# Where the mean, the second pair's products and four centred tiles of a two-block network are kept

## The chip, the cores and the metric

The kernel runs on one core of one Trainium2 chip. The metric is the device time of one execution in microseconds (us), the median of the runs shown. TensorE (PE), VectorE (DVE), ScalarE (ACT), GpSimd (POOL) and SyncE (SP, which issues the transfers) each work off their own list of instructions in order, and meet through semaphores.

## What is computed

512 rows of width 1024 go through a network of two blocks in float32. Cut to what the change touches, the first block's layer, run twice, is:

```
h   = x @ w_in                      # then three mixers: attention, latent attention, RWKV
mix = concatenate([o_sb, o_mla, o_rwkv]) @ w_o
x   = layer_norm(ALPHA * x + mix, ln1_g, ln1_b)
u_act, u_gate = split(x @ ffn_w_up)
x   = layer_norm(ALPHA * x + (gelu(conv(u_act)) * u_gate) @ ffn_w_down, ln2_g, ln2_b)
```

The second block has a recurrent mixer, a pooling mixer and two feed-forward nets behind RMS norms.

## The kernel before

**Layout.** Features lie on the 128 partitions and the 512 rows of x along the free axis, so x is 8 tiles of 128x512. Weights stream from HBM as chunks of 128x1024 (eight 128x128 blocks), in a fixed order, into two slots of `raw`. Each product is made of three passes: a chunk is split by ACT into a high part `wh` (L1560) and by DVE into a low part `wl` (L2392), x likewise into `xh` and `xl`, and `split_product` issues xh·wh, xl·wh, xh·wl (L673 to L675). One chunk is 24 matmuls of 128x512 and one PSUM bank of output. Chunks alternate between the dense banks `dbank[0]` and `dbank[1]`; six more banks are `aux[0]` to `aux[5]`. `bank_free[j]` counts the reads that have freed dense bank j, `lo_done` the chunks whose low part is there, `pe_chunk` the chunks multiplied.

**Norms.** k = 0 to 8 number the norms: 0 and 1 are the layer norms of the first layer, 2 and 3 of the second, 4 to 8 the RMS norms. Norms 0, 1, 2 and 5 are "deferred" (`deferred`): the next product does not wait for the norm.
- `ahead_pair`: the first pair of chunks behind the norm is multiplied with the unnormalised x times the gain, as two parts `hidh`/`hidl` or `xh`/`xl` made by `ahead_hi` on ACT and `ahead_lo` on DVE (L2476), into `aux[0]` and `aux[1]`. After its first four tiles TensorE spreads the sum of x over all partitions (`spread`, L777: the mean, into `MEAN`), and later the sum of squares (into `aux[4]`). `ahead_out` corrects the products by mean and deviation afterwards.
- `turned_pair`: the second pair goes tile by tile over the normalised x, into `TURNED`, which is `(aux[3], dbank[1])`. Tile t waits until its low part is there: tiles 1, 3 and 5 get theirs from GpSimd (`low_parts`, L3354), the rest from DVE (L2527).
- The third pair follows in `turned_pair` too, in dbank[0] and dbank[1]. Its second product waits for all reads of bank 1.
- The fourth pair and the rest are plain `dense` calls.

**The norm's own work.** ACT copies the mean (L1613) to `mean_t` and squares it; DVE takes the mean off each of the 8 tiles (`centre`, L2453, reading the bank `MEAN`), makes the variance (L2443, L2444); ACT makes the root (L1620, L1622, into `aux[4]`, called RSTD). `turned_tiles` on DVE then scales tile by tile (L2517) while ACT makes `xh` (L1659) and the shifted x (L1662).

**The sums.** For norms 0 and 2 DVE adds up x (`tile_sum`, L2995) and its squares (`square_sum`, L3003) between the additions of the mixer's output (L3013), with one `ahead_lo` per tile among them; GpSimd splits four chunks of weights there (`low_weights`, L3361). For norms 1 and 3 GpSimd adds both up (`sum_tiles`, L3371 and L3377), and the squares of norm 5.

## Time and profile before

| | before |
|---|---|
| device time, median of 3 runs | 2390.69 us (2389.5 to 2391.33) |
| the profiled execution: its own time | 2391.46 us |
| the profiled execution: its span, first to last instruction | 2389.5 us |
| mean granted TensorE clock | 0.986 |
| PE busy | 2310.2 us (97%) |
| DVE busy | 1435.3 us (60%) |
| ACT busy | 1030.2 us (43%) |
| POOL busy | 253.8 us (11%) |
| DMA | 248.34 MB, mean 104 GB/s |

Matmuls are pipelined and their ends are modelled, so a busy PE is not PE at its peak. The idle time before an instruction is printed in brackets behind it, with what ended it. Norm 0 lies at 320 to 390 us of the span, norm 1 at 690 to 766, norm 2 at 1036 to 1105, norm 3 at 1430 to 1466, norm 5 at 1620 to 1672.

### The profile page before, as it was taken

What the parts mean: (1) busy time and instruction counts of PE and PEld (TensorE: products, weight loads), DVE (VectorE), ACT (ScalarE), POOL (GpSimd) and SP (SyncE); (2) the same over time, 40 slices, a digit from 0 to 9 for tenths busy, and PEclk for the clock granted to TensorE, in tenths of its full rate; (3) what the DMA queues carried; (4) which work ended last, traced back from release to release, by engine and by line L of the source; (5) the groups of instructions that cost most, each with busy time, mean ns of one, the idle gap of its engine ahead of it and who ended that gap; (6) DMA issues with size and microseconds to landing.
All of it is one profiled execution on the core that took longest, in us unless ns stands there. A gap on an engine that the chain in (4) does not pass through costs nothing.

```text
span 2389.5 us, 35656 instructions
## 1 busy us (share of the span) xinstructions
PE 2310.2 (97%) x13312; PEld 1852.6 (78%) x13312; DVE 1435.3 (60%) x1966; ACT 1030.2 (43%) x1608; POOL 253.8 (11%) x189
## 2 busy tenths in 40 slices
PE   8999999999998999999999998999999999999998
PEld 6777767888886777767888876777888888888887
DVE  4678687666576568686666556587444356533443
ACT  5667255333345657254333334665233243322332
POOL 0041110000042042110000040201000010000001
PEclk9999999999999999999999997999999999999999
DMA  4210014555432210014555431222322221222222
GB/s 161 80 62 28 29 45 158 194 193 193 160 111 72 82 63 28 29 45 159 192 194 193 160 111 39 79 90 97 98 96 96 97 97 62 89 97 97 97 97 88
DMA packets 68797, 248.34 MB, mean 104 GB/s; under 512 B 7632, under 2 KB 8144, under 8 KB 68688
## 3 DMA queue, kind: packets, MB, share of 16 engines
q1 hardware_dynamic: 68688, 246.85, 31.1%
q8 instruction: 72, 1.18, 0.2%
q14 instruction: 37, 0.30, 0.0%
HBM read 244.73 MB, written 2.10 MB: 103 GB/s over the span
## 4 chain that ended last, share of the span: by engine, by line
PE 84%; DVE 8%; ACT 4%; issue 3%; POOL 0%; DMA 0%; DVEq 0%; ACTq 0%; SPq 0%; POOLq 0%
PE dense L673 23%; PE dense L675 23%; PE dense L674 23%; PE aux L673 1%; ACT wh L1560 1%; PE aux L674 1%; PE aux L875 1%; PE aux L675 1%; DVE wl L2392 1%; PE aux L1033 1%; DVE hidl L2476 1%; PE aux L1051 1%; PE aux L1154 1%; PE aux L1165 1%; PE aux L1021 1%
## 5 line engine op out<-in xcount | busy, mean ns | idle before, releaser
L1560 ACT ACTIVATE wh<-raw 128x1024 fp32r<-128x1024 f32 x338 | 358.0, 1059 | 889.0 <-PE dense L675 880.5
L673 PE MATMUL dense<-xh,wh 128*128 128x512 f32 x1744 | 700.4, 402 | 29.4 <-DVE wl L2392 10.5
L675 PE MATMUL dense<-xh,wl 128*128 128x512 f32 x1744 | 682.6, 391 | 0.0
L674 PE MATMUL dense<-xl,wh 128*128 128x512 f32 x1744 | 682.4, 391 | 0.0
L2392 DVE TENSOR_TENSOR wl<-raw,wh 128x1024 fp32r<-128x1024 f32 x330 | 414.9, 1257 | 429.7 <-ACT wh L1560 428.8
L673 PEld LDWEIGHTS dense<-xh,wh 128*128 128x128 f32 x1744 | 329.8, 189 | 118.2 <-issue 42.8
L674 PEld LDWEIGHTS dense<-xl,wh 128*128 128x128 f32 x1744 | 330.0, 189 | 71.1 <-issue 5.8
L675 PEld LDWEIGHTS dense<-xh,wl 128*128 128x128 f32 x1744 | 329.4, 189 | 70.1
L673 PE MATMUL dense<-hidh,wh 128*128 128x512 f32 x928 | 362.9, 391 | 4.9 <-DVE hidl L2427 2.1
L674 PE MATMUL dense<-hidl,wh 128*128 128x512 f32 x928 | 361.2, 389 | 0.0
L675 PE MATMUL dense<-hidh,wl 128*128 128x512 f32 x928 | 361.1, 389 | 0.0
L673 PEld LDWEIGHTS dense<-hidh,wh 128*128 128x128 f32 x928 | 174.2, 188 | 46.6 <-DVE hidl L2427 7.4
L675 PEld LDWEIGHTS dense<-hidh,wl 128*128 128x128 f32 x928 | 174.2, 188 | 36.3
L674 PEld LDWEIGHTS dense<-hidl,wh 128*128 128x128 f32 x928 | 174.2, 188 | 35.7
L3258 DVE SCALAR_TENSOR_TENSOR x<-dense,mod,x 128x512 f32 (+1 forms) x64 | 48.1, 751 | 180.4 <-PE dense L675 180.4
L3377 POOL TENSOR_TENSOR norm_sq<-norm_sq,sq 128x512 f32<-128x512 f32 x38 | 69.1, 1817 | 722.1 <-ACT sq L1599 722.1
L3036 DVE CUSTOM_DVE_ANT_0 mraw<-mraw,cond 128x1024 f32<-128x1024 f32 x96 | 117.1, 1220 | 0.0
L2043 ACT ACTIVATE hidh<-hf 128x512 f32 (+1 forms) x108 | 68.1, 631 | 99.1 <-DVE hf L3234 92.7
L2427 DVE TENSOR_TENSOR hidl<-hf,hidh 128x512 f32 (+1 forms) x108 | 74.5, 690 | 59.8 <-ACT hidh L2043 59.8
L3371 POOL TENSOR_TENSOR norm_sum<-norm_sum,x 128x512 f32<-128x512 f32 x16 | 26.5, 1656 | 492.1 <-DVE x L2951 492.1
L1599 ACT ACTIVATE sq<-x 128x512 f32<-128x512 f32 x64 | 39.9, 624 | 44.5 <-DVE x L3013 16.2
L2693 DVE TENSOR_TENSOR_SCAN later<-keep 128x127 f32<-128x127 f32 (+3 forms) x32 | 34.0, 1062 | 17.1 <-ACT sig L1826 13.3
(450 smaller groups left out, 2669.2 us busy)
## 6 DMA issues: line engine op xcount, KB each, us to landing
raw<-stream SPq DMA_DIRECT2D x362, 512.0 KB, 3.4
mraw<-mod_stream SPq DMA_DIRECT2D x96, 512.0 KB, 4.2
x<-x_t SPq DMA_DIRECT2D x4, 512.0 KB, 6.7
y_t<-x SPq DMA_DIRECT2D x8, 256.0 KB, 2.0
cst<-consts SPq DMA_DIRECT2D x1, 994.0 KB, 9.3
band<-bands SPq DMA_DIRECT2D x1, 576.0 KB, 4.6
cond<-c_rows SPq DMA_DIRECT2D x1, 512.0 KB, 9.9
pv_next<-vecs SPq DMA_DIRECT2D x3, 82.5 KB, 4.6
```

The costliest lines, as they stand in the source:

```text
L673: pe.matmul(o, a, h, start=first, stop=False)
L674: pe.matmul(o, a, l, start=False, stop=False)
L675: return pe.matmul(o, b, h, start=False, stop=last)
L1560: act.activation(wh[:, slot].rearrange("p k m -> p (k m)"), raw[:, slot, :], ACT.Copy).then_inc(hi_done, 1)
L1599: act.activation(sq[:, m % 2, :], x[:, m, :], ACT.Square).then_inc(sq_ready, 1)
L2043: act.activation(hidh[:, slot_i, :], hf[:, j, :], ACT.Copy).then_inc(hidh_ready, 1)
L2392: tt(wl[:, slot].rearrange("p k m -> p (k m)"), raw[:, slot, :], wh[:, slot].rearrange("p k m -> p (k m)").bitcast(F32), SUB)\
L2427: tt(dst, src, hi.bitcast(F32), SUB).then_inc(ready, 1)
L2693: chain(dve.tensor_tensor_scan(later[:, b, 0:n - 1][:, ::-1], k, k, 1.0, MUL, ALU.min))
L3036: dve.tensor_tensor_reduce(mraw[:, j, :], mraw[:, j, :], cond[:], 1.0, 0.0, MUL, ADD, mod_col[:, m:m + 1])\
L3258: stt(x[:, m, :], dbank[j][:], mod[:, lay, bass.ds(40 + m, 1)], x[:, m, :], MUL, ADD).then_inc(bank_free[j], 1)
L3377: pool.tensor_tensor(norm_sq[:], norm_sq[:], sq[:, m % 2, :], ALU.add)\
```

## The change

It moves work between banks and engines; no product is added or left out.
- The mean's spread goes to `dbank[0]`, `TURNED` becomes `(aux[3], aux[5])`. The second product of the third pair no longer waits for the read of the turned pair's second bank, and its first product waits for the four tiles that DVE centres.
- DVE centres tiles 0 to 3 only, two before and two behind the variance. GpSimd centres tiles 4 to 7 (`pool_centred`), from `mean_t`, once all eight ahead low parts are made.
- In norms 0 and 2, DVE makes the ahead low parts of tiles 4 to 7 behind the sums, sums the last tile before the square before it, and splits the last of the four chunks in GpSimd's place.
- In norms 1 and 3, DVE adds the last tile and its square (`last_sum`, `last_square`) in GpSimd's place, in norm 5 the last square.

```diff
--- before.py
+++ after.py
@@ -187,6 +187,7 @@
 IN_PLACE = (1, 5)
 WIDE = (0, 1, 2, 3, 5)
 SUMS = (0, 8, 0, 8, 7, 8, 7, 7, 7)
+LAST_SUM = (1, 3, 5)
 SQ_SUMS = (14, 8, 14, 8)
 STAGE_NORM = (None, 0, 1, 2, 4, None, 5, 7)

@@ -236,6 +237,9 @@
     return sum(1 for d in DEFERRED if d < k and d in IN_PLACE)
+
+
+OWN_CENTRED = 4
@@ -564,8 +569,8 @@
         OUT_AT = {30: 2, 31: 0}
         OUT_ORDER = (2, 0, 1, 3)
         MODS = 24
-        AHEAD, TURNED, COLS = (aux[0], aux[1]), (aux[3], dbank[1]), aux[2]
-        MEAN, RSTD = aux[5], aux[4]
+        AHEAD, TURNED, COLS = (aux[0], aux[1]), (aux[3], aux[5]), aux[2]
+        MEAN, RSTD = dbank[0], aux[4]

         def mod_late(L):

@@ -769,12 +774,12 @@
             def spread(k, square):

                 if k in (0, 2):
-                    pe.wait_ge(sq_added, sq_sums_before(k) + (14 if square else 13))
+                    pe.wait_ge(sq_added, sq_sums_before(k) + (14 if square else 12))
                 elif k < 4 and square:
                     pe.wait_ge(sq_added, sq_sums_before(k) + 8)
                 else:
                     pe.wait_ge(sums_tile, sums_before(k) + 8)
-                pe.matmul(aux[4 if square else 5][:], const("ones"),
+                pe.matmul((aux[4] if square else MEAN)[:], const("ones"),
                           norm_sq[:] if square else norm_sum[:], start=True, stop=True)\
                     .then_inc(sums_pe if square else mean_pe, 1)

@@ -832,8 +837,6 @@
                             pe.wait_ge(lo_half, 2 * q + j + 1)
-                            if j == 1:
-                                pe.wait_ge(bank_free[1], pl.use(s + 1) - 1)
                         if t == 4:
                             pe.wait_ge(lo_done, pl.chunk(s + j) + 1)
                         m = split_product(TURNED[j][:], ((s + j) % 2, t * P), slice(0, P),
@@ -844,7 +847,9 @@
                     pe.wait_ge(lo_half, 2 * (q + 1) + j + 1)
-                    pe.wait_ge(bank_free[j], pl.use(s + j, 1) - 2 + 2 * j)
+                    pe.wait_ge(bank_free[j], pl.use(s + j, 1) - 2)
+                    if j == 0 and k < 4:
+                        pe.wait_ge(centred_x, OWN_CENTRED * (k + 1))
                     for t in range(KT):
                         if t == 4:
@@ -2446,6 +2451,19 @@
+            def last_sum(k):
+
+                dve.wait_ge(*x_added(k, KT - 1))
+                dve.wait_ge(sums_tile, sums_before(k) + KT - 1)
+                tt(norm_sum[:], norm_sum[:], x[:, KT - 1, :], ADD).then_inc(sums_tile, 1)
+
+            def last_square(k):
+
+                dve.wait_ge(sq_ready, 8 * k + KT)
+                added = (sq_added, sq_sums_before(k)) if k < 4 else (sums_tile, sums_before(k))
+                dve.wait_ge(added[0], added[1] + KT - 1)
+                tt(norm_sq[:], norm_sq[:], sq[:, 1, :], ADD).then_inc(added[0], 1)
+
@@ -2502,24 +2520,24 @@

             def turned_tiles(k, g, b, pl, s, q):

-                lead = 6
-                for m in range(4):
+                for m in range(2):
                     centre(k, m)
                 variance_tile(k)
+                for m in range(2, OWN_CENTRED):
+                    centre(k, m)
                 for j in range(2):
                     early_half(q, j)
-                for m in range(4, lead):
-                    centre(k, m)
                 dve.wait_ge(rstd_ready, norms_scaled(k) + 1)

                 def scale(m):
-                    dve.wait_ge(centred_x, 8 * k + m + 1)
+                    if m < OWN_CENTRED:
+                        dve.wait_ge(centred_x, OWN_CENTRED * k + m + 1)
+                    else:
+                        dve.wait_ge(centred_pool, (KT - OWN_CENTRED) * k + m - OWN_CENTRED + 1)
                     stt(x[:, m, :], x[:, m, :], vec(g, m), RSTD[:], MUL, MUL).then_inc(n_mul, 1)

                 scale(0)
                 for m in range(KT):
-                    if m + lead < KT:
-                        centre(k, m + lead)
                     if m + 1 < KT:
                         scale(m + 1)
                     if m not in POOL_LOW:
@@ -2538,7 +2556,7 @@
-                    dve.wait_ge(centred_x, 8 * k + m + 1)
+                    dve.wait_ge(centred_x, OWN_CENTRED * k + m + 1)
@@ -2999,7 +3017,7 @@
                     dve.wait_ge(sq_ready, 8 * k + m + 1)
                     if m > 1:
-                        dve.wait_ge(sq_added, sq_sums_before(k) + 2 * m - 2)
+                        dve.wait_ge(sq_added, sq_sums_before(k) + (13 if m == KT - 1 else 2 * m - 2))
                     tt(norm_sq[:] if m == KT - 1 else aux[4][:], sq[:, m % 2, :],
@@ -3011,14 +3029,19 @@
                             dve.wait_ge(pe_chunk, pl.chunk(C_WO + 4 + a) + 1)
                         m = 2 * a + e
                         tt(x[:, m, :], x[:, m, :], dbank[e][:], ADD).then_inc(bank_free[e], 1)
-                        if m >= 2:
+                        if 2 <= m < KT - 1:
                             square_sum(m - 1)
                         if m:
                             tile_sum(m)
+                        if 1 <= m < 5:
                             ahead_lo(k, m - 1, vec("ln1_g", m - 1))
+                up = C_FFN[0][0]
+                square_sum(KT - 2)
+                dve.wait_ge(lo_done, pl.chunk(up + 1))
+                refill(pl, C_WO + 7)
                 square_sum(KT - 1)
-                up = C_FFN[0][0]
-                ahead_lo(k, KT - 1, vec("ln1_g", KT - 1))
+                for m in range(4, KT):
+                    ahead_lo(k, m, vec("ln1_g", m))
                 turned_tiles(k, "ln1_g", "ln1_b", pl, up, q)
                 ahead_out(k, pl, up, 0, vec("conv2", 0))
                 for j in range(2):
@@ -3085,7 +3108,11 @@
                             residual(pl, down + j, i, i * 2 + j, g == 0)
+                            if g == 2 and i == 3 and j == 1:
+                                last_sum(k2)
                             refill(pl, down + j, i)
+                            if g == 2 and i == 3 and j == 1:
+                                last_square(k2)
                             if g == 2 and k2 in DEFERRED:
@@ -3204,6 +3231,8 @@
+                    if m == KT - 1:
+                        last_square(5)
@@ -3354,6 +3383,14 @@
+            def pool_centred(k):
+
+                pool.wait_ge(mean_ready, 2 * k + 1)
+                pool.wait_ge(xl_ready, lows_before(k, True))
+                for m in range(OWN_CENTRED, KT):
+                    pool.tensor_tensor(x[:, m, :], x[:, m, :], mean_t[:], ALU.subtract)\
+                        .then_inc(centred_pool, 1)
+
@@ -3364,7 +3401,7 @@
-                for m in range(SUMS[k]):
+                for m in range(SUMS[k] - (k in LAST_SUM)):
                     if k < 4:
@@ -3449,13 +3486,15 @@
                     masked(lkT, b, "tri_incl", lbk_masked)
                 clear_sums(L * 2, mixl_ready, L * 8 + 8, True)
                 pool.memset(ua[:, 0:3], 0.0).then_inc(ua_zero, 1)
-                for a in range(4):
+                for a in range(3):
                     n = place1(L).chunk(C_WO + 6 + a)
                     low_weights(n, a % 2)
+                pool_centred(L * 2)
                 low_parts(L * 2)
                 clear_sums(L * 2 + 1, n_aff, L * 16 + 8, True)
                 sum_tiles(L * 2 + 1)
                 if L == 0:
+                    pool_centred(1)
                     low_parts(1)

             def gated_inputs():
```

Three places in the order of the instructions are shown. Line numbers of the changed kernel are some lines higher for the same statement.

TensorE, the turned pair of norm 0 (tile 0's last two passes into aux3, then tile 0 of the second chunk), and the starts of the third pair's two products; before:

```order
L675 MATMUL aux3<-xh_51,wl_55 128x512
L673 MATMUL dense1<-xh_51,wh_54 128x512 [waits bank1_read,lo_half]
...
L673 MATMUL dense0<-xh_51,wh_54 128x512 [waits bank0_read,lo_half]
...
L673 MATMUL dense1<-xh_51,wh_54 128x512 [waits bank1_read,lo_half]
```

and now:

```order
L680 MATMUL aux3<-xh_51,wl_55 128x512
L678 MATMUL aux5<-xh_51,wh_54 128x512 [waits lo_half]
...
L678 MATMUL dense0<-xh_51,wh_54 128x512 [waits centred_x,bank0_read,lo_half]
...
L678 MATMUL dense1<-xh_51,wh_54 128x512 [waits bank1_read,lo_half]
```

The last row reads alike in both; the count that it waits for is two reads lower now.

VectorE, norm 0, from the addition of the mixer's last tile to the first scaled tile; before:

```order
L3013 TENSOR_TENSOR x_50<-x_50,dense1 128x512 [waits pe_chunk]
L3003 TENSOR_TENSOR aux4<-sq_69,aux4 128x512 [waits sq_added,sq_ready]
L2995 TENSOR_TENSOR norm_sum_67<-x_50,aux3 128x512 [waits bank1_read,sq_added]
L2476 SCALAR_TENSOR_TENSOR hidl_124<-x_50,pv_57,hidh_123 128x512 [waits xh_ready]
L3003 TENSOR_TENSOR norm_sq_68<-sq_69,aux4 128x512 [waits sq_added,sq_ready]
L2476 SCALAR_TENSOR_TENSOR hidl_124<-x_50,pv_57,hidh_123 128x512 [waits xh_ready]
L2453 SCALAR_TENSOR_TENSOR x_50<-aux5,x_50 128x512 [waits mean_ready]
L2453 SCALAR_TENSOR_TENSOR x_50<-aux5,x_50 128x512 x3
L2443 SCALAR_TENSOR_TENSOR var_t_73<-aux4,var_t_73 128x512 [waits sums_pe,mean_ready]
L2444 TENSOR_SCALAR var_t_73<-var_t_73 128x512 [waits dve_chain]
L2405 TENSOR_TENSOR wl_55<-raw_53,wh_54 128x512 [waits hi_half] x2
L2453 SCALAR_TENSOR_TENSOR x_50<-aux5,x_50 128x512 x2
```

and now:

```order
L3031 TENSOR_TENSOR x_50<-x_50,dense1 128x512 [waits pe_chunk]
L3013 TENSOR_TENSOR norm_sum_67<-x_50,aux3 128x512 [waits bank1_read,sq_added]
L3021 TENSOR_TENSOR aux4<-sq_69,aux4 128x512 [waits sq_added,sq_ready]
L2397 TENSOR_TENSOR wl_55<-raw_53,wh_54 128x1024 [waits hi_done,lo_done]
L3021 TENSOR_TENSOR norm_sq_68<-sq_69,aux4 128x512 [waits sq_added,sq_ready]
L2494 SCALAR_TENSOR_TENSOR hidl_124<-x_50,pv_57,hidh_123 128x512 [waits xh_ready] x4
L2471 SCALAR_TENSOR_TENSOR x_50<-dense0,x_50 128x512 [waits mean_ready]
L2471 SCALAR_TENSOR_TENSOR x_50<-dense0,x_50 128x512
L2448 SCALAR_TENSOR_TENSOR var_t_73<-aux4,var_t_73 128x512 [waits sums_pe,mean_ready]
L2449 TENSOR_SCALAR var_t_73<-var_t_73 128x512 [waits dve_chain]
L2471 SCALAR_TENSOR_TENSOR x_50<-dense0,x_50 128x512 x2
L2410 TENSOR_TENSOR wl_55<-raw_53,wh_54 128x512 [waits hi_half] x2
```

The sum of x is one instruction behind the last addition instead of two; four low parts and one chunk's low weights stand between it and the first centred tile, and the variance stands behind two centred tiles instead of four.

GpSimd, norm 0, behind the mixers; before:

```order
L3361 TENSOR_TENSOR wl_55<-raw_53,wh_54 128x1024 [waits lo_done,hi_done] x4
L3354 TENSOR_TENSOR xl_52<-x_50,xh_51 128x512 [waits n_aff] x3
```

and now:

```order
L3398 TENSOR_TENSOR wl_55<-raw_53,wh_54 128x1024 [waits lo_done,hi_done] x3
L3391 TENSOR_TENSOR x_50<-x_50,mean_t_71 128x512 [waits xl_ready,mean_ready]
L3391 TENSOR_TENSOR x_50<-x_50,mean_t_71 128x512 x3
L3383 TENSOR_TENSOR xl_52<-x_50,xh_51 128x512 [waits n_aff] x3
```

Four centrings stand ahead of its three low parts, in the place of one chunk.

## Rows read from the trace of the kernel before

**Rows 1.** Page, part 1: busy us (share of the span) xinstructions.

```profile
PE 2310.2 (97%) x13312; PEld 1852.6 (78%) x13312; DVE 1435.3 (60%) x1966; ACT 1030.2 (43%) x1608; POOL 253.8 (11%) x189
```

**Rows 2.** Who TensorE waited for, whole span: us in total, times, longest us.

```profile
PE dense L673 <- DVE hf L3078: 8.2, 2, 4.1
PE dense L673 <- ACT sbq L1760: 5.0, 1, 5.0
PE aux L777 <- POOL norm_sum L3371: 3.1, 2, 2.1
PE aux L777 <- DVE norm_sum L2995: 2.1, 2, 1.1
```

**Rows 3.** Third pairs, PE timeline: start us, us, engine, line, work [idle before <-releaser].

```profile
379.66 0.77 PE L673 MATMUL dense<-xh,wh 128*128 128x512 f32 x1 [4.11 <-DVE hf L3078]
755.68 0.76 PE L673 MATMUL dense<-xh,wh 128*128 128x512 f32 x1 [5.02 <-ACT sbq L1760]
1668.29 0.47 PE L673 MATMUL dense<-xh,wh 128*128 128x512 f32 x1 [1.86 <-ACT gel L2312]
```

**Rows 4.** Busy time by stretch: us, PE, PEld, DVE, ACT, POOL, PEclk, DMA share, GB/s.

```profile
379.66:384.45 4.79, 4.79 (x11) 3.77 (x12) 4.39 (x6) 1.56 (x3) 0.00 (x0) 0.51 0.32 109
755.68:759.65 3.97, 3.97 (x9) 3.10 (x10) 1.33 (x1) 1.28 (x2) 3.20 (x4) 0.50 0.15 38
1095.40:1101.10 5.70, 5.67 (x13) 4.46 (x14) 4.39 (x6) 1.59 (x4) 0.00 (x0) 0.50 0.31 98
```

**Rows 5.** Timeline of what a fourth pair needs, norms 0, 1 and 5.

```profile
380.12 0.59 ACT L2102 ACTIVATE ua<-dense 128x512 f32<-128x512 f32 x1
379.68 1.23 DVE L2392 TENSOR_TENSOR wl<-raw,wh 128x1024 fp32r<-128x1024 f32 x1 [0.16 <-ACT wh L1560]
756.51 1.33 DVE L2392 TENSOR_TENSOR wl<-raw,wh 128x1024 fp32r<-128x1024 f32 x1 [1.03 <-ACT wh L1560]
765.22 1.13 PE L929 MATMUL aux<-csq,cst 128*128 128x512 f32 x2
1670.63 1.22 DVE L2392 TENSOR_TENSOR wl<-raw,wh 128x1024 fp32r<-128x1024 f32 x1 [0.26 <-ACT wh L1560]
```

**Rows 6.** Timeline of the mean, norm 0: VectorE, TensorE.

```profile
343.81 0.68 DVE L2995 TENSOR_TENSOR norm_sum<-x,aux 128x512 f32<-128x512 f32 x1
344.54 0.70 PE L777 MATMUL aux<-norm_sum,cst 128*128 128x512 f32 x1 [1.05 <-DVE norm_sum L2995]
```

**Rows 7.** Timeline of GpSimd and, behind the row of rows 6, VectorE.

```profile
343.14 2.36 POOL L3361 TENSOR_TENSOR wl<-raw,wh 128x1024 fp32r<-128x1024 f32 x1 [3.46 <-ACT wh L1560]
344.40 1.65 DVE L2476 SCALAR_TENSOR_TENSOR hidl<-x,pv,hidh 128x512 fp32r<-128x512 f32 x1
```

**Rows 8.** Timeline, norm 0: variance, first scaled tile, first GpSimd low part.

```profile
351.19 0.43 DVE L2444 TENSOR_SCALAR var_t<-var_t 128x512 f32<-128x512 f32 x1
353.94 0.74 DVE L2517 SCALAR_TENSOR_TENSOR x<-x,pv,aux 128x512 f32<-128x512 f32 x1
357.38 1.29 POOL L3354 TENSOR_TENSOR xl<-x,xh 128x512 fp32r<-128x512 f32 x1 [11.88 <-ACT x L1662]
```

**Rows 9.** Timeline, norm 0: the two waits of TensorE in the turned pair.

```profile
358.73 0.50 PE L673 MATMUL aux<-xh,wh 128*128 128x512 f32 x1 [0.42 <-POOL xl L3354]
362.45 0.60 PE L821 MATMUL aux<-cst,rows_t 4*128 4x2 f32 x4 [0.70 <-POOL xl L3354]
```

**Rows 10.** Timeline, last tile sums and what follows, norms 1 and 3.

```profile
717.48 2.26 POOL L3371 TENSOR_TENSOR norm_sum<-norm_sum,x 128x512 f32<-128x512 f32 x1
719.79 0.70 PE L777 MATMUL aux<-norm_sum,cst 128*128 128x512 f32 x1 [0.97 <-POOL norm_sum L3371]
1433.10 1.26 POOL L3371 TENSOR_TENSOR norm_sum<-norm_sum,x 128x512 f32<-128x512 f32 x1 [0.56 <-DVE x L2951]
1434.32 2.24 POOL L3377 TENSOR_TENSOR norm_sq<-norm_sq,sq 128x512 f32<-128x512 f32 x1
1438.18 0.60 ACT L1613 ACTIVATE mean_t<-aux 128x512 f32<-128x512 f32 x1
```

1 line of the change is left out of this document (added).

## The prediction

> **What bounds the kernel now.** I read the page first. TensorE is busy for 2310.2 us of a span of 2389.5 us [rows 1], so the end moves only if TensorE's idle time goes or if its matmuls run at a higher clock. The second view is the list of what TensorE waited for. Three of its rows name reads of the bank in which the turned pair leaves its second product: 8.2 us in two waits on `hf` and 5.0 us in one wait on `sbq` [rows 2]. The third view, TensorE's own timeline, shows where: each wait stands ahead of the second product of a third pair, 4.11 us in norm 0, 5.02 in norm 1 and 1.86 in norm 5 [rows 3]. Norm 2 repeats norm 0: the two waits on `hf` sum to 8.2, so 4.1 again. The weights are not what is waited for there; the matmul waits because dbank[1] still holds the turned pair's product. The fourth view, stretches of the timeline, shows what comes behind: in the 4.79 us after the wait of norm 0 the granted clock is 0.51, in 3.97 us of norm 1 it is 0.50, in 5.70 us of norm 2 it is 0.50 [rows 4]. That is the level of 1.2 GHz, half of the 2.4 GHz at which TensorE ran before its idle time. So a wait of 4 or 5 us is paid for twice. Further waits are small: 3.1 us and 2.1 us for the sum of x [rows 2], and two in norm 0's turned pair, 0.42 and 0.70 [rows 9].
>
> **1. TURNED in two auxiliary banks.** The second product of the third pair no longer waits for `hf`, `sbq` or `gel`. Gross: 4.11 + 5.02 + 4.1 + 1.86 = 15.1 us. It then starts when the first one ends, at 379.66 - 4.11 = 375.6 in norm 0. What is late next? The fourth pair needs two things: its weights' low part and a free dbank[0]. A product is 24 matmuls. At half clock one took 3.97 / 9 = 0.44 us [rows 4], so at full clock 0.22 and 5.3 us for 24; in norm 0 the second product would be through at 375.6 + 5.3 = 380.9. The low part is finished at 379.68 + 1.23 = 380.9, the last read of dbank[0] at 380.12 + 0.59 = 380.7 [rows 5]. Neither depends on the removed wait, as the chunk's slot was freed by the first product. That is a tie: at most some tenths are left. In norm 1 the low part is there at 756.51 + 1.33 = 757.8 [rows 5], while the product ends at 755.68 - 5.02 + 5.3 = 756.0; but the sums of squares of the latent attention (L926 to L929) stand between them on TensorE. The last ended at 766.35 [rows 5]; the product ahead of them ran from 755.68, nine matmuls in 3.97 us and fifteen at 0.22, to about 763.0. So they take some 3 us and cover the 1.8. In norm 5: 1670.63 + 1.22 = 1671.9 against 1668.29 - 1.86 + 5.3 = 1671.7 [rows 3, 5], a tie again. I take 0.3 us of new waits in all; the bounds are 0 and 1.5 us at each of the four places, if ScalarE or VectorE are held up by an instruction more. Net 14.8 us.
>
> **2. The clock behind these waits.** Without the idle time the stretches run at the upper level: 4.79 x 0.49 + 3.97 x 0.50 + 5.70 x 0.50 = 7.2 us [rows 4]. The wait of norm 5 counts nothing here: the matmul behind it takes 0.47 us as printed against 0.77 and 0.76 behind the long ones [rows 3]. Bounds: 7.2, and 0 if the clock falls for another reason nearby.
>
> **3. The mean of norms 0 and 2, earlier.** TensorE waits 1.05 us for the sum [rows 6]. Now one instruction instead of two, and no low part between the last two additions, stands ahead of it on VectorE: the low part alone took 1.65 us there [rows 7]. The sum is ready some 2 us earlier and the wait goes, so everything behind it on TensorE comes 1.05 us sooner. Whether that is kept depends on the first normalised tile. GpSimd starts its four centrings when VectorE has made the eighth low part. Counted from the sum, which ended at 344.5 [rows 6] and is some 2.3 us earlier now, that is 342.2 + 0.6 (square) + 1.2 (weights) + 0.6 (square) + 4 x 0.65 (low parts) = 347.2. It needs 4 x 1.29 us (the nearest subtraction of one tile) [rows 8], until 352.4. In that time VectorE takes the variance. An instruction of VectorE with two operands in SBUF was held until GpSimd's ended: GpSimd's ran 343.14 to 345.50, VectorE's low part stood from 344.40 to 346.05 and is otherwise one of 0.7 us [rows 7], while the sum from 343.81, with one operand in PSUM, took its usual 0.68 beside it [rows 6]. Centrings on VectorE read PSUM and are not held. The two halves of `wl` are: the first waits for the last centring. L2444 is the unknown, one operand in SBUF and 0.43 us for 512 columns [rows 8]; no row shows it beside GpSimd. Bounds: 0 as with the PSUM operand, and one whole instruction of 1.29. I take about 1 us, since its speed, 0.43 against 0.68 for the others, tells that it is a different kind of access. Then VectorE is free for the first scaling at 353.9, as in the row [rows 8], and no sooner: held `wl` and L2444 eat what four centrings (4 x 0.6 us) fewer give back. TensorE, 1.05 us early, waits some 0.6 there, and the waits for GpSimd's low parts, 0.42 and 0.70, become near 0.4 and 1.0 [rows 9]. Kept: 0.65 us at each of two norms, 1.3 us. Bounds: 1.8 each (about 1.05 and both waits), and a loss of 0.7 each, if a second held instruction adds its 1.29.
>
> The Trainium skill (SBUF — State Buffer, "Who interferes with whom") states that `tensor_scalar` can take the port pair that VectorE and GpSimd share, and then blocks fully. By that rule it is held, the sum has the 1.3 us above; without it 2.2 us. No row here shows it.
>
> **4. The same in norms 1 and 3.** GpSimd's last addition of x ran until 717.48 + 2.26 = 719.74 in norm 1 and TensorE waited 0.97 us for it [rows 10]. On VectorE it takes 0.7 us once GpSimd's square before it has ended, near 717.5. The wait of 0.97 goes. GpSimd is idle then, starts its centrings at the mean, about 720.6, and is through with them near 725.8, before VectorE needs the port for `wl`. So the gain is kept and the four centrings less help: 1.2 us. Bounds 0.5 and 2. In norm 3 nothing is deferred and the chain is serial: GpSimd's last square ended at 1434.32 + 2.24 = 1436.6, and the modulation's sum, a table load and `mean_t` at 1438.18 came behind it [rows 10]. With both on VectorE this is over by 1435.3: 1.2 us. In norm 5 the square was not waited for: 0.
>
> **5. What costs nothing.** The chunk's low part on VectorE instead of GpSimd (1.23 us for the same shape [rows 5]) lies in the time that VectorE waited for the mean; were that gone, the second ahead product would start up to 1 us late. The new wait for four centred tiles ahead of dbank[0] is met over 10 us before. No transfer is moved; the loads follow the low parts and go with them.
>
> **Sum.** 14.8 + 7.2 + 1.3 + 1.2 + 1.2 = 25.7 us. From the profiled execution's own 2391.46 us (its span and 1.96 us around it) that gives 2365.8; the median of the runs lies 0.77 us below it, so the forecast is 2365.0 us.
>
> **Rivals.**
> - *The wait moves on.* VectorE's or ScalarE's list is too full behind the third pair and TensorE waits at the fourth pair instead, in norms 0, 1 and 2. For it: the ties of part 1. Against it: both sides of the tie stand in rows that don't depend on the wait [rows 5]. If half of each wait is found again and the clock with it: 25.7 - 7.5 - 3.6 = 14.6 us, 2376 us.
> - *The clock falls in the turned pair.* Three waits of 0.4 to 1.0 us within 6 us in norms 0 and 2 bring the lower level: a stretch of 5 us at half clock costs 2.4 us twice. Against it: 1.05, 0.42 and 0.70 lay there before, at full clock. 2370 us.
> - *Slower: GpSimd's four centrings hold VectorE's port.* Place: between the mean and the second scaling of norms 0, 1 and 2. Four instructions of VectorE can be held (L2444, the two halves of `wl`, the low part of tile 0). If each waits 2.3 us, as long as GpSimd's own take when VectorE is in their way [rows 10], that is 9.2 us, less 2.4 for the four centrings that VectorE is rid of: the turned pair starts 6.8 us late, TensorE's clock falls for 2.4 us more, and three times 9.2 is 27.6 us against the 14.8 + 7.2 + 1.2 = 23.2 us that stay: 4.4 us slower, 2395 us. It decides from 1.9 us per held instruction in all three norms. Against it: the row has 1.29 for GpSimd alone [rows 8], and its four are over before the low part of tile 0.
> - *It doesn't do what it says.* The second product waits for another read of bank 1. The order of the instructions speaks against it: its count is lower by the two reads.
>
> **Chances.** Forecast 0.79, the wait moves on 0.07, clock in the turned pair 0.08, slower 0.03, not as it says 0.03. A measurement of this kernel tells 0.2%, 4.8 us, from no change. All but the last two lie beyond it on the faster side: faster 0.94, same 0.03, slower 0.03. The range takes in the bounds of parts 3 and 4 (some 3.5 us more gain, some 3.5 less) and 1 us of new waits at each of three fourth pairs, and with that the second rival: 2361 to 2372 us.
>
> **What would show it.** In the profile after, no wait ahead of a third pair's second product, and a granted clock near 1.0 in the 5 us behind; waits of some tenths at the fourth pair. GpSimd's centrings at 1.3 us each, ended before the second half of `wl`; L2444 longer than 0.43 in norms 0 and 2 and not by much in norm 1; the mean's spread without a wait in norms 0 to 2; norm 3's `mean_t` 1.2 us nearer to the last product. The forecast is wrong if a wait over 2 us stands at the fourth pair, or at the first tile of the turned pair.

## The result, and the profile after

The changed kernel takes 2365.49 us (median of 4 runs, 2362.47 to 2368.51) against 2391.01 us for the kernel before (4 runs): ratio 0.9894, 95% interval 0.9877 to 0.9912, 25.5 us less. A second timing on another occasion gave 2363.73 us (4 runs) against 2389.73 us (7 runs), 0.9893 (0.9876 to 0.9909). The forecast was 2365.0 us. The profiled execution took 2367.96 us, its span is 2366.0 us.

| | before | after |
|---|---|---|
| span, us | 2389.5 | 2366.0 |
| TensorE busy, us | 2310.2 | 2301.9 |
| mean granted clock | 0.986 | 0.991 |

The page of the changed kernel, part 1, answers to [rows 1]:

```profile
PE 2301.9 (97%) x13312; PEld 1848.0 (78%) x13312; DVE 1428.6 (60%) x1961; ACT 1029.7 (44%) x1608; POOL 257.6 (11%) x194
```

Busy and idle time both fell: 8.3 us of busy time with the same number of matmuls, which is clock, and 15.2 us of idle time (23.5 - 8.3). Four rows of what TensorE still waited for (us in total, times, longest) answer to [rows 2]:

```profile
PE dense L678 <- DVE wl L2397: 12.7, 10, 8.6
PE aux L880 <- ACT sq L1604: 5.9, 1, 5.9
PE dense L782 <- DVE norm_sum L2458: 1.5, 1, 1.5
PE aux L678 <- DVE xl L2545: 1.4, 2, 0.7
```

The `hf` and `sbq` rows are gone, and of `gel` 0.6 us is left, a wait elsewhere. The longest `wl` wait, 8.6 us (8.3 before), stands at the program's start in both kernels. One row has grown, 5.9 us for a square in norm 3 (3.2 before), which matters below, and one is new, 1.4 us for the first normalised tile. The stretches that answer to [rows 4], and one more of the same view (us; PE, PEld, DVE, ACT, POOL busy; PEclk; DMA share; GB/s):

```profile
374.00:380.00 6.00, 6.00 (x27) 4.69 (x25) 4.78 (x7) 4.82 (x9) 0.00 (x0) 1.00 0.50 183
741.00:747.00 6.00, 6.00 (x28) 4.96 (x27) 2.05 (x3) 4.90 (x10) 0.88 (x4) 1.00 0.05 18
1076.00:1082.00 6.00, 6.00 (x29) 4.95 (x28) 4.20 (x7) 4.61 (x8) 0.00 (x0) 1.00 0.68 223
...
794.00:804.00 10.00, 9.61 (x26) 6.69 (x27) 8.46 (x12) 5.75 (x10) 0.00 (x0) 0.66 0.21 63
```

TensorE is busy through each third pair's second product, at full clock. The last row is a dip that the kernel before doesn't have in its profile. To see where the time went I compared when both kernels reach the same instruction of TensorE. Three of these rows of the kernel before, then the same of the changed one:

```profile
737.55 0.60 PE L821 MATMUL aux<-cst,rows_t 4*128 4x2 f32 x4 [0.69 <-POOL xl L3354]
810.45 0.47 PE L673 MATMUL aux<-lora_in_h,wh 64*128 64x512 f32 x1 [0.83 <-issue]
1460.93 2.05 PE L882 MATMUL aux<-cst,stat 128*128 128x128 f32 x8 [2.13 <-DVE stat L2436]
```

```profile
728.79 0.60 PE L826 MATMUL aux<-cst,rows_t 4*128 4x2 f32 x4 [0.49 <-POOL xl L3383]
794.39 0.47 PE L678 MATMUL aux<-lora_in_h,wh 64*128 64x512 f32 x1 [0.83 <-issue]
1439.70 2.05 PE L887 MATMUL aux<-cst,stat 128*128 128x128 f32 x8 [2.13 <-DVE stat L2441]
```

| point | before | after | lead | won since the point above |
|---|---|---|---|---|
| norm 0, last wait of the turned pair | 362.45 | 361.54 | 0.91 | 0.91 |
| norm 1, the same | 737.55 | 728.79 | 8.76 | 7.85 |
| layer 1, low-rank products | 810.45 | 794.39 | 16.06 | 7.30 |
| norm 2, as in norm 0 | 1078.21 | 1064.30 | 13.91 | -2.15 |
| norm 3, first row of 1/rms | 1460.93 | 1439.70 | 21.23 | 7.32 |
| norm 5, as in norm 0 | 1653.16 | 1631.80 | 21.36 | 0.13 |
| last norm but one | 2022.40 | 1999.42 | 22.98 | 1.62 |
| last norm | 2380.53 | 2357.02 | 23.51 | 0.53 |

The row with the minus sign holds the dip: from the first low-rank matmul to the first dense one behind them it is 12.4 us instead of 9.4, all of it clock, with the same 0.83 us of idle time ahead of them in both. The 0.53 of the last row is a dip of the kernel before right behind its last norm but one (granted clock 0.63 from 2022 to 2025 us, 1.00 at the same place in the changed one).

### The profile page after: what moved, and what is told of

Read it like the earlier page. It is cut to its first block, busy times and chain, and to the rows that moved or that the text cites. A ratio compares the mean times of both kernels' runs of the same rounds, so it can differ in the third digit from the quotient of the medians.

```text
span 2366.0 us, 35655 instructions
## 1 busy us (share of the span) xinstructions
PE 2301.9 (97%) x13312; PEld 1848.0 (78%) x13312; DVE 1428.6 (60%) x1961; ACT 1029.7 (44%) x1608; POOL 257.6 (11%) x194
## 4 chain that ended last, share of the span: by engine, by line
PE 86%; DVE 6%; ACT 4%; issue 2%; DMA 0%; POOL 0%; DVEq 0%; ACTq 0%; SPq 0%
PE dense L678 24%; PE dense L680 23%; PE dense L679 23%; PE aux L678 1%; PE aux L679 1%; PE aux L680 1%; PE aux L880 1%; ACT wh L1565 1%; DVE wl L2397 1%; PE aux L1038 1%; PE aux L1056 1%; PE aux L1159 1%; PE aux L1170 1%; PE aux L1026 1%; PE aux L1255 1%
## 5 line engine op out<-in xcount | busy, mean ns | idle before, releaser
L678 PE MATMUL dense<-xh,wh 128*128 128x512 f32 x1712 | 685.1, 400 | 15.5 <-DVE wl L2397 10.9
L680 PE MATMUL dense<-xh,wl 128*128 128x512 f32 x1712 | 668.2, 390 | 0.0
L679 PE MATMUL dense<-xl,wh 128*128 128x512 f32 x1712 | 667.7, 390 | 0.0
L678 PEld LDWEIGHTS dense<-xh,wh 128*128 128x128 f32 x1712 | 322.3, 188 | 102.8 <-issue 26.3
L679 PEld LDWEIGHTS dense<-xl,wh 128*128 128x128 f32 x1712 | 322.4, 188 | 69.4 <-issue 5.8
L680 PEld LDWEIGHTS dense<-xh,wl 128*128 128x128 f32 x1712 | 322.0, 188 | 67.9
L3414 POOL TENSOR_TENSOR norm_sq<-norm_sq,sq 128x512 f32<-128x512 f32 x35 | 63.4, 1810 | 717.1 <-ACT sq L1604 717.1
```

Of the source, the lines that this page charges most:

```text
L678: pe.matmul(o, a, h, start=first, stop=False)
L679: pe.matmul(o, a, l, start=False, stop=False)
L680: return pe.matmul(o, b, h, start=False, stop=last)
L3414: pool.tensor_tensor(norm_sq[:], norm_sq[:], sq[:, m % 2, :], ALU.add)\
```

## Experiments

Each kernel was timed against the kernel before in the same series. Medians of neighbouring versions differ by less than their runs scatter (some 5 us), so parts of 1 or 2 us are read from the traces, as the distance between two points of TensorE's timeline.

**1. The banks alone.** The kernel before with

```
-        AHEAD, TURNED, COLS = (aux[0], aux[1]), (aux[3], dbank[1]), aux[2]
-        MEAN, RSTD = aux[5], aux[4]
+        AHEAD, TURNED, COLS = (aux[0], aux[1]), (aux[3], aux[5]), aux[2]
+        MEAN, RSTD = dbank[0], aux[4]
```

and TensorE's waits as in the change (`centred_x` at 8 per norm).

> The kernel before with the two banks alone: the turned pair in aux[3] and aux[5], the mean in dbank[0], TensorE's waits to match; VectorE centres all eight tiles, the sums and the low parts stay where they were. My theory: parts 1 and 2 of the prediction stand by themselves, 14.8 us of idle time and 7.2 us of clock, so 2391.0 - 22.0 = 2369 us; no wait at a third pair's second product in norms 0, 1, 2 and 5, the mean's wait of 1.05 us as before. Rival: the wait moves on, because VectorE's list, which still has all eight centrings, is too full at the fourth pair: half of it is found again there, about 2380 us, and a wait of 1.5 to 2.5 us stands ahead of a dense product behind each third pair.

Measured: 2368.9 us, ratio 0.9908 (0.9893 to 0.9923), 21.5 us below the 2390.44 us of its series. Its waits:

```profile
PE dense L777 <- POOL norm_sum L3371: 3.1, 2, 2.1
PE dense L777 <- DVE norm_sum L2995: 2.1, 2, 1.1
```

The waits for the sum of x stay as in [rows 2]; no `hf`, no `sbq`. The fourth pair starts at 380.39 in norm 0, 0.44 us behind the start of the third pair's last matmul (0.23 is the usual distance). Parts 1 and 2 stand alone, and the rival that moves the wait on is out, even with all eight centrings on VectorE.

**2. The rest alone.** The changed kernel with the banks and waits of before (the diff above, reversed).

> The changed kernel with the banks of before (turned pair in aux[3] and dbank[1], mean in aux[5], TensorE's old waits). My theory: parts 3 and 4 alone, 3.7 us in the prediction, about 4 us by the trace of the changed kernel: 2387 us, the third pairs' waits 4.1, 5.0, 4.1 and 1.9 us as before. Rival: the reads of dbank[1] come from a list of VectorE and ScalarE that doesn't move with TensorE, so that what is won ahead of the third pair is waited for in it: no change, 2391 us, and the waits are longer by 0.7 in norms 0 and 2 and by 1.6 in norm 1.

Measured: 2384.59 us, ratio 0.9979 (0.9970 to 0.9988), 5.9 us less than before.

```profile
PE dense L678 <- DVE hf L3101: 8.2, 2, 4.1
...
PE dense L678 <- ACT sbq L1765: 5.0, 1, 5.0
```

The waits have kept their length: the reads of dbank[1] move with TensorE, and nothing of parts 3 and 4 is swallowed. The two halves add up to 21.5 + 5.9 = 27.4 us, against 25.5 and 26.0 for the whole. The 5.9 are more than the 3.7 forecast. At least part of that is clock: the first matmuls behind the wait of norm 0 run at half clock from 379.33 to 382.32 only, 7 of them, against 11 in [rows 4].

**3. Matmuls in the third pair's wait.** The kernel before, whose waits stay:

```
                 for j in range(2):
+                    if j == 1 and k < 4:
+                        pe.wait_ge(centred_x, 8 * (k + 1))
+                        for _ in range(5 if k == 1 else 4):
+                            pe.matmul(aux[5][:], const("ident"), cst[:, 0:S], start=True, stop=True)
```

> The kernel before with matmuls into an idle bank (aux[5]) in the third pair's wait: 8 of 0.47 us, 3.8 us, in norms 0 and 2, 10, 4.7 us, in norm 1; their results are not used. The idle time stays as long as it is, only the clock behind it is at stake. My theory: part 2 is a term of its own, so 7.2 us come off and no more: 2391.0 - 7.2 = 2383.8 us, with a granted clock near 1.0 in the 5 us behind each third pair's wait. Rival: the clock falls there for another reason, or comes back as slowly: 2391 us, clock 0.5. Third case: the fill outlasts the wait and costs what it saves: waits gone and the second product later than 379.66 us.

Measured: 2385.1 us, ratio 0.998 (0.9971 to 0.9989), 5.3 us less than before. The fill and what is left of the wait, then two stretches:

```profile
374.89 3.60 PE L849 MATMUL aux<-cst 128*128 128x512 f32 x8
379.15 0.47 PE L673 MATMUL dense<-xh,wh 128*128 128x512 f32 x1 [0.66 <-DVE hf L3082]
```

```profile
379.00:384.00 5.00, 4.85 (x22) 4.06 (x23) 4.39 (x7) 1.71 (x4) 0.00 (x0) 1.00 0.32 105
752.00:758.00 6.00, 5.27 (x24) 4.34 (x24) 1.96 (x2) 2.11 (x4) 3.27 (x4) 1.00 0.26 89
```

The second product starts 4.49 us after the last matmul of the first has started (379.15 - 374.66), exactly as late as with the idle wait (379.66 - 375.17), and now at full clock; in norms 1 and 2 the two distances agree within 0.01 us as well, so the fill itself costs nothing. The clock is a term of its own, and it is the idle time ahead that brings it down. Of the 7.2 us expected 5.3 are seen. Other dips, below, add or take: this profile has two (0.86 over 8 us at 1578, 0.83 over 10 us at 1658) where the one of before has 1.00, about 1.1 and 1.7 us.

**4. All eight centrings on VectorE.** The changed kernel with

```
-OWN_CENTRED = 4
+OWN_CENTRED = 8
...
-                pool_centred(L * 2)
```

and tiles 4 and 5 behind the halves of `wl`, 6 and 7 among the scalings.

> The changed kernel with all eight centrings of norms 0, 1 and 2 on VectorE again, tiles 0 to 3 ahead of the two halves of wl, 4 and 5 behind them, 6 and 7 among the scalings; everything else stays. My theory: in norms 0 and 2 GpSimd's help is almost nothing, as its centrings hold the two halves of wl for 1.1 us (2.37 us in the changed kernel, 1.28 before) and the four that VectorE is rid of are 4 x 0.63 = 2.5 us, of which only 1.3 lie ahead of the first scaling. The first scaling comes at 354.0 instead of 353.8, and the later ones by two centrings later: the last wait of norm 0's turned pair (361.54 in the changed kernel) ends 0.2 to 0.5 us later. With norm 1 the same, some 1 us in all: 2366.5 us. Rival: the centrings on GpSimd carry parts 3 and 4; without them the earlier mean is lost at the first normalised tiles, about 0.7 us in norm 0, 1.0 in norm 2 and 1.6 in norm 1: 2369 us.

Measured: 2368.11 us, ratio 0.9909 (0.9895 to 0.9922). VectorE in norm 0, the changed kernel first:

```profile
349.85 0.54 DVE L2449 TENSOR_SCALAR var_t<-var_t 128x512 f32<-128x512 f32 x1
350.31 1.27 DVE L2471 SCALAR_TENSOR_TENSOR x<-dense,x 128x512 f32<-128x512 f32 x2
351.51 2.37 DVE L2410 TENSOR_TENSOR wl<-raw,wh 128x512 fp32r<-128x512 f32 x2
353.80 1.39 DVE L2537 SCALAR_TENSOR_TENSOR x<-x,pv,aux 128x512 f32<-128x512 f32 x2
```

```profile
349.72 0.43 DVE L2449 TENSOR_SCALAR var_t<-var_t 128x512 f32<-128x512 f32 x1
350.06 1.28 DVE L2471 SCALAR_TENSOR_TENSOR x<-dense,x 128x512 f32<-128x512 f32 x2
351.26 1.29 DVE L2410 TENSOR_TENSOR wl<-raw,wh 128x512 fp32r<-128x512 f32 x2
352.46 1.28 DVE L2471 SCALAR_TENSOR_TENSOR x<-dense,x 128x512 f32<-128x512 f32 x2
353.66 1.40 DVE L2539 SCALAR_TENSOR_TENSOR x<-x,pv,aux 128x512 f32<-128x512 f32 x2
```

TensorE, the same kernel, a wait that the changed one hasn't:

```profile
365.33 0.51 PE L678 MATMUL aux<-xh,wh 128*128 128x512 f32 x1 [0.36 <-POOL xl L3387]
```

Beside GpSimd the two halves of `wl` take 2.37 us instead of 1.29; the centrings with their PSUM operand take the same; L2449 takes 0.11 more. So the first scaling comes as early either way in norm 0. From the start of the first ahead product to the last wait of the turned pair it is 21.09 us in norm 0, 20.79 in norm 1, 20.79 in norm 2, against 21.13, 20.01 and 20.78 in the changed kernel, and a further wait of 0.36 to 0.38 us follows in all three. The distance that takes in this wait, to the first matmul of the third pair, is 29.24, 28.97 and 28.98 us against 28.61, 27.48 and 28.27 in the changed kernel, and 29.32, 29.08 and 29.27 in run 1, which has neither part 3 nor part 4. So GpSimd's help is worth 0.6, 1.5 and 0.7 us, 2.8 in all (the medians of the two kernels lie 2.6 apart); without it 0.1, 0.1 and 0.3 us are left of what the changed kernel wins there. My theory of 1 us was too low, and the rival, by which the centrings on GpSimd carry the gain of parts 3 and 4 in these norms, is nearly right.

**5. Six tiles on GpSimd.** The changed kernel with `OWN_CENTRED = 2`.

> The changed kernel with six tiles centred by GpSimd (2 to 7) instead of four. It doses the prediction's slower rival. My theory: GpSimd's list runs from 347.6 for 6 x 1.3 to 1.45 us, until 356 or so in norm 0. VectorE saves two centrings (1.3 us) ahead of the halves of wl, which are held as before (2.4 us for both), and the first scaling could start near 352.5; the low part of tile 0, with two operands in SBUF, is now held too, up to 1.3 us. The two about cancel: the first wait of the turned pair (356.13 in the changed kernel) moves by -0.7 to +0.5 us, and the kernel by no more than 1.5 us: 2364 to 2367. Rival, by the prediction's slower case: each VectorE instruction with two operands in SBUF waits out a whole centring of GpSimd, three instead of two of them, and each centring is itself stretched to 2.3 us: the turned pairs start 3 us later, 2374 us.

Measured: 2367.35 us, ratio 0.9902 (0.9887 to 0.9918). GpSimd and VectorE in norm 0:

```profile
348.64 8.59 POOL L3391 TENSOR_TENSOR x<-x,mean_t 128x512 f32<-128x512 f32 x6 [8.07 <-DVE hidl L2494]
```

```profile
351.38 3.47 DVE L2410 TENSOR_TENSOR wl<-raw,wh 128x512 fp32r<-128x512 f32 x2
...
356.30 1.48 DVE L2545 SCALAR_TENSOR_TENSOR xl<-x,pv,xh 128x512 fp32r<-128x512 f32 x1
```

The halves take another 1.1 us and the low part of tile 0 is held for 0.7 (0.75 in the changed kernel). The distances are 21.56, 21.06 and 21.21 us: 0.4 to 1.1 us more than with four tiles. The rival's mechanism is real and far from its price: a centring takes 8.59 / 6 = 1.43 us, not 2.3.

**6. The sums back on GpSimd.** The changed kernel with `LAST_SUM = ()` and without the calls of `last_sum` and `last_square`.

> The changed kernel with GpSimd adding the last tiles of norms 1, 3 and 5 again. My theory: in norm 1 the wait for the mean is back, 0.97 us, and what stands behind it is late by as much, less what the turned pair's waits of 0.21 and 0.49 give back; in norm 3 mean_t comes 1.02 us later after the last down-product, of which 0.6 reach the end; norm 5 doesn't change. Together 1.2 to 1.7 us slower than the changed kernel: 2367 us. Rival: the late mean costs 1.2 us in norm 1 and as much in norm 3, as the prediction had it, and the clock falls behind the waits: 2369 us or more.

Measured: 2367.58 us, ratio 0.99 (0.9884 to 0.9915). In norm 1 the distance is 21.07 us against 20.01, and the wait of 0.97 us is back: 1.06 us. In norm 3 the sum is waited for 2.12 us and the square 1.07, as before, against 1.50 and 0.61. Norm 1 came out as expected; norm 3 didn't. From the last matmul of the last down-product to the first row of 1/rms it is 29.44 us here and 28.42 in the changed kernel, so all of the 1.02 us reach the rows, where I expected 0.6.

**7. The low parts between the sums.** The changed kernel with

```
-                        if 1 <= m < 5:
+                        if m:
                             ahead_lo(k, m - 1, vec("ln1_g", m - 1))
...
-                for m in range(4, KT):
-                    ahead_lo(k, m, vec("ln1_g", m))
+                ahead_lo(k, KT - 1, vec("ln1_g", KT - 1))
```

> The changed kernel with the mixers' low parts of tiles 0 to 6 each behind its tile's sum again, ahead of the next residual addition, and the one of tile 7 behind the last square (norms 0 and 2). My theory: this is what won part 3. The low parts of tiles 4 to 6 stand ahead of the last sum on VectorE, 0.66 us each, and one of them at least between the last two additions: the mean's wait of 1.05 us is back in part (0.3 to 1.05 us), in two norms; but the low parts are through sooner by as much, so that GpSimd starts its centrings no later. Slower than the changed kernel by 0.3 to 1.5 us: 2366.5 us. Rival: VectorE's list ahead of the mean has room, since it waits there for the last residual product; no change, 2365.5 us, the spread of the mean without a wait.

Measured: 2368.51 us, ratio 0.991 (0.9893 to 0.9926). TensorE in norm 0:

```profile
343.34 1.12 PE L782 MATMUL dense<-norm_sum,cst 128*128 128x512 f32 x2 [0.65 <-DVE norm_sum L3013]
345.73 0.50 PE L678 MATMUL aux<-hidh,wh 128*128 128x512 f32 x1 [1.27 <-DVE wl L2397]
```

Two stretches of TensorE, norm 0 behind these waits and norm 2 behind the same two, 0.65 and 1.27 us:

```profile
346.00:352.00 6.00, 6.00 (x29) 4.38 (x29) 3.45 (x6) 1.15 (x2) 4.92 (x4) 1.00 0.26 87
1047.00:1052.00 5.00, 4.99 (x17) 3.81 (x18) 2.41 (x4) 0.04 (x1) 3.64 (x3) 0.66 0.31 105
```

The mean is waited for 0.65 us, and then the second ahead product waits 1.27 us more, for the weights' low part that the change has put on VectorE. The distance is 22.68 us against 21.13 in the changed kernel and 21.84 before. The order of the low parts is worth 1.5 us in norm 0; the chunk's low part on VectorE is free only behind it. In norm 2 it is 23.84 us against 20.78, 3.1 us, and some 1.7 of these are clock: 0.66 over 5 us, where norm 0 kept 1.00 behind the same waits. Both are more than the 0.3 to 1.5 us that I expected of the two norms together; the wait of 1.27 us was not in it.

**8. More spare matmuls in norm 3.** The changed kernel with 16 instead of 4 (`range(8)` for `range(spare)` behind `spread(k, True)`).

> The changed kernel with 12 more of the spare matmuls of norm 3 (16 instead of 4, 0.47 us each; their results are not used), over the 5.90 us in which TensorE waits there for the first square. My theory: the half clock that follows in norm 3 (64 matmuls of the sums in 13.9 us, then 2.6 us for the rows of 1/rms) comes from this wait alone. With it filled the sums go at ScalarE's pace of 1.28 us a tile, some 3 us sooner, the rows take 1.3 us instead of 2.6, and the first product behind them saves 0.5: 4.9 us less than the changed kernel, 2360.6 us. Rival: at full clock TensorE waits between the tiles and the clock falls all the same: no change against the changed kernel, 2365.5 us. Third case: the fill ends after the first square is there and the norm starts later: up to 1 us more.

Measured: 2363.98 us, ratio 0.9889 (0.9874 to 0.9904).

```profile
1413.83 7.03 PE L911 MATMUL aux<-cst 128*128 128x512 f32 x16
1421.61 1.10 PE L880 MATMUL aux<-cst,sq 128*128 128x64 f32 x8 [0.74 <-ACT sq L1604]
...
1425.43 8.79 PE L880 MATMUL aux<-cst,sq 128*128 128x64 f32 x40 [0.17 <-ACT sq L1604]
```

My theory fell. Three tiles of sums ran at full clock, then the clock dropped all the same: 1.00 until 1425, 0.52 behind. The wait was one cause, not the only one. From the mean's matmul to the rows of 1/rms it is 25.2 us against 26.5, so 1.3 us won of the 4.9 expected.

**9. And one small matmul behind each tile's sums.** The kernel of 8 with

```
                         add(1, sq[:, m % 2, :], m == 0, m == KT - 1, aux[3])\
                             .then_inc(sums_tile if m < KT - 1 else sums_pe, 1)
+                        pe.matmul(aux[0][:, 0:P], const("ident"), cst[:, 0:P], start=True, stop=True)
```

> The changed kernel with the 16 spare matmuls of norm 3, as in the run before, and one more of 128x128x128 (0.24 us, from 0.94 for 512 columns) behind the sums of each of norm 4's eight tiles. In the run before, the clock fell in the sums themselves, 3.8 us after they had begun at full clock, though TensorE idled there only 0.17 us a tile. My theory: it falls because the sums' matmuls are short (8 columns each, 0.14 us) and leave the engine's array mostly unused, whatever the busy share says; a small dense matmul per tile isn't enough to keep it, so the clock falls again and the fillers add 8 x 0.24 to 0.48 us in part: 0 to 2 us slower than the run before (2364.0). Rival: the idle 0.17 us per tile brings it down; with it filled the sums run through at 1.34 us a tile, the rows behind at full clock, and some 4 us come off: 2360.

Measured: 2360.23 us (2358.05 to 2361.02), ratio 0.9873 (0.9858 to 0.9888). Its stretches of norm 3, and one of them in 8:

```profile
1420.00:1425.00 5.00, 4.25 (x34) 3.88 (x33) 5.00 (x10) 4.87 (x9) 0.00 (x0) 1.00 0.02 3
1425.00:1432.00 7.00, 6.18 (x50) 5.66 (x48) 2.25 (x5) 5.44 (x9) 0.10 (x1) 1.00 0.00 0
1432.00:1440.00 8.00, 6.96 (x24) 4.62 (x25) 5.54 (x9) 3.50 (x6) 0.00 (x0) 0.79 0.00 0
```

```profile
1425.00:1432.00 7.00, 6.83 (x34) 6.69 (x34) 2.82 (x5) 5.34 (x9) 0.10 (x1) 0.52 0.00 0
```

The rival was right: the sums now go at their producers' pace of 1.27 us a tile, at full clock, and from the mean's matmul to the rows it is 22.65 us, 3.9 less than in the changed kernel. (The sums' matmuls have 64 columns, not 8 as I wrote.) Whether the filler works by closing the 0.17 us gaps or by the denser work that it is, these runs don't separate. The Trainium skill (TensorE: Matmul & The Clock Gate, "A second HAM failure mode: psum-queue depth-cycling") has a kernel in which frequent short idle times between groups of matmuls bring the clock down. Run 8, with 0.17 us of idle time a tile, fits that, but doesn't show that the idle time is the cause.

**10. The small matmuls without the 12 others.**

> The changed kernel with the small matmul behind each of norm 4's eight tiles of sums, without the 12 further spare matmuls in the 5.90 us ahead of them. With both the clock stayed up in norm 3 and the kernel took 2360.2 us; with the 12 alone it fell in the sums, 2364.0 us. My theory: both are needed. The wait of 5.90 us brings the clock down before the sums begin, as in the changed kernel; at half clock the sums and their fillers take 1.7 + 0.5 us a tile, some 4 us more in all: 2368 to 2370 us. Rival: the idle time among the sums does it, and the small matmuls alone hold the clock or bring it back: 2361 us.

Measured: 2366.85 us, ratio 0.9898 (0.9882 to 0.9915).

```profile
1421.67 1.97 PE L880 MATMUL aux<-cst,sq 128*128 128x64 f32 x8 [5.89 <-ACT sq L1605]
```

The wait of 5.89 us is whole, the sums begin at half clock and stay there; the norm takes 29.5 us from the mean's matmul to the rows, 3.0 more than in the changed kernel. Both fills are needed: the small ones alone cost 3.0 us in this norm, the 12 others alone (run 8) win 1.3, both together 3.9.

**11. A fill in the wait for `ga_lower` too.** The kernel of 9 with

```
+                    if n == 6:
+                        pe.wait_ge(bank_free[0], pl.use(C_Y))
+                        for _ in range(3):
+                            pe.matmul(dbank[0][:], const("ident"), cst[:, 0:S], start=True, stop=True)
```

> The changed kernel with both fills in norm 3 (16 spare matmuls, the small ones among the sums) and 6 of 0.47 us into dbank[0], 2.8 us, in the wait of 2.90 us for ga_lower behind the RG-LRU's sixth gate tile. Behind this wait the changed kernel has a stretch at half clock that costs 3.4 us; the version with the two fills had the same wait of 2.90 us and no dip in its profile. My theory: the dip there comes in some executions only, 1.7 to 3.4 us; filled, it never comes, and the median lies 1 to 2 us below 2360.2. Rival: what holds the clock up there is the fill in norm 3, further ahead: 2360.2 us, no difference. Third case: the fill is late by some tenths and costs them.

Measured: 2358.81 us (2357.85 to 2361.30), ratio 0.9872 (0.9856 to 0.9889); against run 9's 0.9873 that is no difference that these runs can tell. The wait shrank from 2.90 to 0.32 us behind the fill. Whether the fill earns anything stays open.

**12. The changed kernel once more.**

> The changed kernel itself, once more. Its four runs lay in two pairs, 2362.5 and 2363.0, 2368.0 and 2368.5, and the traces of the study show clock dips of 1.7 or 3.4 us that come in one execution and not in the next (the low-rank products' at 795 us in the changed kernel, at 93 us in others). My theory: that is what the runs scatter by, so they fall between 2362 and 2369 again, median near 2365.5, and the profile has its dips at other places of the same kind. Rival: the place of the dip at 795 us belongs to this kernel, and it is there again.

Measured: 2363.73 us (2361.83 to 2366.08), ratio 0.9893 (0.9876 to 0.9909). This profile's stretches at the two places where the first one had dips (0.66 and 0.83):

```profile
794.00:804.00 10.00, 10.00 (x46) 7.45 (x45) 9.59 (x13) 7.38 (x16) 0.00 (x0) 1.00 0.25 79
...
1495.00:1515.00 20.00, 16.78 (x73) 13.20 (x72) 6.04 (x7) 17.73 (x27) 8.95 (x6) 1.00 0.31 104
```

No dip at either, with the waits ahead of them unchanged. The span is 2359.9 us, 6.1 less than the first profile's, for the same instructions. These dips belong to the execution, not to the kernel.

## Why the prediction was right

**Part 1 and 2** (14.8 and 7.2, 22.0 us). The trace gives, norm by norm: norm 0 7.85 less the 1.60 of norm 1's mean, 6.25; norm 1 7.30; norm 2 6.72 (of the 7.32 of its row, 0.60 are norm 3's); norm 5 1.62. Together 21.9, and run 1 has 21.5. Run 3 shows the clock as a separate term. The ties at the fourth pairs came out as ties: the one row with a wait is norm 5's, 0.17 us. The latent sums covered norm 1's low part.

**Part 3** (0.65 us in each of two norms). The mean's wait went, and the distance from the ahead product to the turned pair's last wait fell by 0.71 us in norm 0 and 1.06 in norm 2. The sum was right; two terms in it were not. L2449 (L2444 before) was to be held for 1 us in norm 0 and took 0.54 instead of 0.43, and in norm 1, where I expected little, it took 0.82. It is held all the same, until the centring that GpSimd has in work is over. The rows of it and of GpSimd, norm 1 of the changed kernel and norm 0 of run 7:

```profile
717.90 0.82 DVE L2449 TENSOR_SCALAR var_t<-var_t 128x512 f32<-128x512 f32 x1
713.42 5.03 POOL L3391 TENSOR_TENSOR x<-x,mean_t 128x512 f32<-128x512 f32 x4 [3.09 <-DVE xl L2494]
...
351.38 1.04 DVE L2449 TENSOR_SCALAR var_t<-var_t 128x512 f32<-128x512 f32 x1
347.08 5.05 POOL L3390 TENSOR_TENSOR x<-x,mean_t 128x512 f32<-128x512 f32 x4 [8.19 <-DVE hidl L2494]
```

GpSimd's last centring ends at 718.45 and 352.13, L2449 at 718.72 and 352.42, 0.3 us behind it in both. In norm 0 of the changed kernel L2449 came some 0.25 us before the end of GpSimd's second centring (347.57 + 2 x 1.26, against 349.85), so it lost only 0.1: the mechanism of my term was right, and its size there depended on where in a centring it fell, which I had not worked out. In norm 2 of run 7, with GpSimd's four over before it, it took 0.43. The rule of the Trainium skill (SBUF — State Buffer, "Who interferes with whom"), by which a `tensor_scalar` can take the shared pair of ports and the engine that comes second then blocks fully, agrees with these rows. The other term is GpSimd's four centrings: 5.76 us in norm 0 instead of 5.2. They take 5.03 where no half of `wl` falls among them (norm 1); in norm 0 the last one took 1.83 beside the first half, and the second half 1.77 instead of 0.7, so they did not end before it, as I had written. The turned pair's waits moved too: 0.72 at tile 0 (0.6 forecast), then 0.19 and 0.55, where I had 0.4 and 1.0:

```profile
356.13 0.50 PE L678 MATMUL aux<-xh,wh 128*128 128x512 f32 x1 [0.72 <-DVE xl L2545]
357.99 0.50 PE L678 MATMUL aux<-xh,wh 128*128 128x512 f32 x1 [0.19 <-POOL xl L3383]
361.54 0.60 PE L826 MATMUL aux<-cst,rows_t 4*128 4x2 f32 x4 [0.55 <-POOL xl L3383]
```

And I credited the mean and the centrings without weighing which did it. Runs 4 and 7 take each back alone: the order of the low parts costs 1.5 us in norm 0, GpSimd's centrings 0.6, against 0.7 won. Neither makes the gain without the other.

**Part 4** (1.2 and 1.2 us). Norm 1 gave 1.60, since four centrings less also shortened the turned pair's waits: 1.5 of it go without them (run 4), 1.1 with the sums back on GpSimd (run 6). Norm 3 gave 0.60. The step before it was right: counted from the last down-product, `mean_t` comes 1.02 us earlier (1.2 forecast). The rest was lost in the sums, which now run at half clock from their start: 64 matmuls in 13.91 us against 13.48.

```profile
1423.66 13.91 PE L880 MATMUL aux<-cst,sq 128*128 128x64 f32 x64 [5.90 <-ACT sq L1604]
```

Moving the additions did not do this. Run 1, with both of them on GpSimd, has 13.92 us behind a wait of 5.85, and run 6 13.91 behind 4.15; against these two the changed kernel is 1.03 and 1.02 us earlier at the rows. It is the kernel before that is the exception: its clock was at 0.50 from 1437 to 1442, in its spare matmuls, and at 0.93 in the 4 us behind, when the sums began. The clock in norm 3 was in no term of mine.

**Part 5** held, and run 7 shows its one condition at work: with the mean no longer the last thing waited for, the chunk's low part on VectorE is late by 1.27 us if other work stands ahead of it.

**The sum.** 21.9 + 1.8 + 2.2 = 25.9 us by the trace, 25.7 forecast. The profiled execution shows 23.5, because its dip at 795 us cost 3.0 us and one of the kernel before, behind its last norm but one, gave 0.5 back. That scatter between executions was in no term of mine; it fell within the range. The terms held, but that the median came within 0.5 us of the forecast is in part luck: its four runs spread over 6 us, and the second timing gave 1.8 us less.

**The rivals.** Run 1 excludes the wait that moves on; the clock stayed at 1.00 in the turned pairs of the changed kernel, though norm 2 of run 7, with waits of 0.65 and 1.27 us, shows that it can fall near there; run 5 shows how much the held port costs per tile (0.2 to 0.5 us), far from the point at which the slower rival decides.

## What to carry to other kernels

A wait ahead of a dense stretch may cost twice, once as idle time and once as half clock behind it; spare matmuls in the wait, left in for one run, tell the two apart. Work moved to an idle engine is worth what the port leaves of it: GpSimd took over four tiles, and in norm 0 the first scaling came no sooner, since it held as much as it took off VectorE; the 0.6 us that it won came behind the first scaling. A gain of 1 us at one point, followed to the next, may shrink: norm 3 was 1.0 us earlier at its mean and 0.6 behind its sums, because the clock in the sums differed; it takes a run with the one part taken back (run 6: 1.0) to see what the part itself is worth.
